# Splitting the weights of a hybrid model: half of the remainder pieces subtracted by GpSimd in the three mixers

## The chip, the cores and the metric

One of the eight cores of a Trainium2 chip runs the whole program. The metric is the device time of one execution in microseconds (us), lower is better; the times shown are medians of several runs on the chip.

## What is computed

Two stacks of layers run one after the other on a sequence of 256 tokens with 1024 features. Everything is 32-bit floating point. A layer is a feed-forward block, a mixer, and another feed-forward block:

```python
x = x + 0.5 * swiglu(rms_norm(x, ffn1_norm), w_gate, w_up, w_down)      # 1024 -> 2816 -> 1024
x = x + mixer(rms_norm(x, mix_norm), ...)
x = x + 0.5 * swiglu(rms_norm(x, ffn2_norm), w_gate, w_up, w_down)
```

The first stack has one layer, whose mixer joins a dilated attention in three groups with an RWKV-7 recurrence over 16 heads (projections, a state of 64x64 per head, normalisation, gates). The second stack has two layers, whose mixer joins three kinds of attention: with relative positions (6 heads), over the 256 best tokens by an index score (5 heads), and over a low-rank latent (5 heads). Each mixer begins with one wide projection of x and ends with a projection back to 1024 features.

## The kernel before

**Matrix products in three passes.** TensorE multiplies in a 32-bit format of reduced precision (fp32r). So each operand is written as high part plus remainder, and a product is three matmuls into the same bank: high x high, high x remainder, remainder x high (`mm3`, L1109 to L1111). The high part of the weights is `whi`, the remainder `wlo`; for the activations they are `xh`, `xl` and `yh`, `yl`.

**Chunks of weights.** The function `plan` cuts all weights into 271 chunks of at most 128 x 2048 values, in the order of use. A chunk goes through these steps:
- SP loads it into one of three buffers `raw` (L1092), as soon as the chunk three before has been split.
- ScalarE copies it, piece by piece, to `whi`, which rounds it to fp32r (L1607). `whi` and `wlo` have two buffers, so this waits until TensorE has used the chunk two before.
- VectorE subtracts, `wlo = raw - whi` (L1925), each piece as soon as ScalarE has done it.
- TensorE uses the chunk. Before its first matmul it waits for the last remainder piece of it.

A chunk is split in two pieces (in the feed-forward blocks, and where nothing is interleaved) or in four.

**The order of the work** is one list of steps, `P.steps`, built in Python by the class `Order`. Each engine walks through the same list and takes the steps for which it has a function; on one engine everything runs strictly in this order, and between engines semaphores tell when a step is done. A step `("split", i, q, n)` lets ScalarE do piece q of chunk i and VectorE subtract piece q - 1, so that VectorE's subtraction "q" is the q-th, from 1 to n. The pieces of chunk i + 1 are spread over the steps in which chunk i is used (`pump`, `pieces`).

**The other work of the mixers.** VectorE does the rotary embeddings (`rope`, L2015 to L2019, products of two tensors in SBUF), masks, row maxima, the triangular solves of the recurrence between TensorE's 64x64 products, the sums of the index scores (L2292 to L2308) and the top-k (L2318, L2321). ScalarE reads the results of matmuls out of PSUM and computes exponentials. GpSimd has the small things: it clears buffers (L2420, L2462, L2484, L2515), computes reciprocal square roots as a power (L2408, L2457, L2475), scales the gates (L2429), copies some rows (L2499 to L2509), and starts a few loads (L2418, L2443, L2468, L2481). The three mixers are the stages "mix1" and, for the second stack, "mix2" with l = 0 and l = 1; their chunks carry the owner "mix1", 0 or 1. Names of chunks such as "qkv", "gate", "in2", "uq", "ukv" are those of `plan`.

Of the kernel before, what the change touches and what calls it, by code (L numbers as in the profile page):

```python
# [291 lines left out]
class Order:  # L292


    def __init__(self, stages):
        self.chunks = plan(stages)
        self.steps = []
        self.bank = Slots(range(8))
        self.slots = {}
        self.n_dma = self.n_split = self.n_use = 0  # L300
        self.under_way = []
        for _ in range(3):
            self.feed_dma()
        self.feed_split()
        for s, st in enumerate(stages):
            if st[0] == "ffn":
                self.ffn(s, st[1])
            elif st[0] == "mix1":
                self.mix1(s)
            elif st[0] == "mix2":  # L310
                self.mix2(s, st[1])
            else:
                self.do("final", s, st[1])
        self.do("out", len(stages))
# [14 lines left out]
    def pieces(self, n):  # L329
        i = self.n_split  # L330
        if i >= len(self.chunks):
            return
        for q in range(n + 1):
            self.do("split", i, q, n)
            if q < n:
                yield 1
        self.n_split += 1
        self.feed_dma()
        yield 1
# [501 lines left out]
def build(nc, stages, x_in, wall, consts, cols, rows, lorap, ebias, out):  # L841
# [3 lines left out]
    offs = np.cumsum([0] + [128 * c[3] for c in P.chunks])  # L845
    with ExitStack() as ctx:
        M = Marks(nc, ctx)
        for name in ("pe", "act", "dve", "pool", "whi", "wlo"):
            M.add(name)
        for name in ("x", "consts", "cols", "raw0", "raw1", "raw2", "masks", "gbias", "bias0", "bias1", "lora0",  # L850
                     "lora1", "rows0", "rows1", "rows2", "gain0", "gain1", "out"):
# [131 lines left out]
        def bank_free(tile):  # L983
            return M.freed(P.bank.at[tile][1])
# [75 lines left out]
        def mus(sid):  # L1060
# [2 lines left out]
            i = "kvr".index(sid[0])  # L1063
            return [3 + 8 * i + 2 * sid[1], 4 + 8 * i + 2 * sid[1]]

        def hbuf(m):
            return yh[:, m % 5, :], yl[:, m % 5, :]

# [11 lines left out]
        def sync_program(e):  # L1080
            due = lambda *t: M.due("sp", *t)
            e.dma_start(X[:], x_in.rearrange("(t p) d -> p t d", p=128)).then_inc(*M.sig("x", ("x",)))
            e.dma_start(C[:], consts[:, 0:cbase]).then_inc(*M.sig("consts", ("c",)))
            e.dma_start(COL[:], cols).then_inc(*M.sig("cols", ("c",)))

            def load(i):
                w = P.chunks[i][3]
                src = wall[int(offs[i]):int(offs[i + 1])].rearrange("(p w) -> p w", p=128)
                if i >= 3:
                    for t in due(("wlo", ("split", i - 3))):  # L1090
                        e.wait_ge(*t)
                e.dma_start(raw[i % 3][:, 0:w], src).then_inc(*M.sig(f"raw{i % 3}", ("chunk", i)))  # L1092

            def out_(s):
                for tt in range(2):
                    for t in due(x_ready(s, tt)):
                        e.wait_ge(*t)
                    e.dma_start(out[tt * 128:(tt + 1) * 128], X[:, tt, :]).then_inc(*M.sig("out", ("out", tt)))
                for t in due(("out", ("out", 1))):
                    e.wait_ge(*t)  # L1100

            run("sp", {"load": load, "out": out_})

        def tensor_program(e):
# [30 lines left out]
            def gu(s, m, i):  # L1135
                hi, lo = whi[i % 2], wlo[i % 2]
                b = bank(("gu", s, m))
                for t in due(("wlo", ("split", i)), bank_free(("gu", s, m))):
                    e.wait_ge(*t)
                for g in range(2):  # L1140
                    for k in range(8):
# [7 lines left out]
            def rows_mm(name, acc, s, j, kk, tt, i, first, last, end, a, b, kper, *toks):  # L1149
                hi, lo = [t[:, 0:1024 * kper].rearrange("p (k n) -> p k n", k=kper) for t in (whi[i % 2], wlo[i % 2])]  # L1150
                for nn in range(2):
                    tile = (acc, s, 2 * tt + nn)
                    for t in due(("wlo", ("split", i)), first and bank_free(tile), *toks):
                        e.wait_ge(*t)
                    c = slice(nn * 512, nn * 512 + 512)
                    p = mm3(bank(tile), a, b, hi[:, kk, c], lo[:, kk, c], first, last)
# [29 lines left out]
            def proj(s, name, j, k, tt, i, nk, w, end):  # L1186
# [1 line left out]
                kk = k % nk  # L1188
                tile = (name, s, j, tt)
                c = slice(tt * 128, (tt + 1) * 128)  # L1190
                for t in due(("wlo", ("split", i)), ("dve", ("xl", s, k - k % 2)), k == 0 and bank_free(tile)):
                    e.wait_ge(*t)
                p = mm3(bank(tile)[:, 0:w], xh[:, k, c], xl[:, k, c], hi[:, kk * w:(kk + 1) * w],
                        lo[:, kk * w:(kk + 1) * w], k == 0, k == 7)
# [3 lines left out]
            def shift_mm(s, sid, j, k0, i, n, w, end):  # L1198
                b = bank(sid)
                for k in range(k0, k0 + 4):  # L1200
                    c0 = k * n * w + j * w
                    for t in due(("wlo", ("split", i)), ("dve", ("xl", s, k - k % 2)), bank_free(sid)):
                        e.wait_ge(*t)
                    p = mm3(b[0:w, j * 256:(j + 1) * 256], whi[i % 2][:, c0:c0 + w], wlo[i % 2][:, c0:c0 + w],
                            xh[:, k, :], xl[:, k, :], k == 0, k == 7)
# [263 lines left out]
            def latent_up(s, nm, tt, c0, i, end):  # L1469
                nk, k0, w, _ = latent_cols(nm)  # L1470
                cw = w if w <= 512 else w // 2
                b = bank((nm, s, tt, c0))
                for t in due(("wlo", ("split", i)), ("dve", ("lat", s, 0 if nm == "uq" else 1)),
                             bank_free((nm, s, tt, c0))):
                    e.wait_ge(*t)
                for k in range(nk):
# [434 lines left out]
        def vector_program(e):  # L1911
# [5 lines left out]
                return M.last("dve")  # L1917

            def split(i, q, n):
                if q:  # L1920
                    w = P.chunks[i][3]
                    c = slice(w * (q - 1) // n, w * q // n)
                    for t in due(("whi", ("split", i, q - 1))):
# [474 lines left out]
        def gpsimd_program(e):  # L2398
# [11 lines left out]
            def sumsq(s, tt):  # L2410
                rstd(small[:, tt:tt + 1], 1, 1024, 1e-6, ("act", ("sumsq", s, tt)), ("rstd", s, tt))

            def m1_begin(s):
                for t in due(*marked("norm", s)):
                    e.wait_ge(*t)
# [101 lines left out]
            def final(s, row):  # L2517
# [4 lines left out]
                for tt in range(2):  # L2522
                    sumsq(s, tt)

            run("pool", {"sumsq": sumsq, "m1_begin": m1_begin, "proj_out": proj_out, "rw_begin": rw_begin,
                         "r_begin": r_begin, "r_scan": r_scan, "r_nrm": r_nrm, "r_xz": r_xz, "r_yp": r_yp,
                         "r_var": r_var, "m2_begin": m2_begin, "lat_sq": lat_sq, "latent_rope": latent_rope,
                         "index_rope": index_rope, "ak_zero": ak_zero, "final": final})
# [135 lines left out]
```

## Time and profile before

| what | value |
|---|---|
| median of 3 runs | 2159.14 us (2157.56 to 2161.05) |
| the profiled execution, its own time | 2152.94 us |
| its span in the trace | 2151.1 us |
| busy: TensorE matmul / weight load | 1935.6 us (90%) / 1751.6 us (81%) |
| busy: VectorE / ScalarE / GpSimd | 1149.3 us (53%) / 927.7 us (43%) / 101.5 us (5%) |
| mean granted clock of TensorE | 0.951 of full speed |

Busy time counts from the start to the end of each instruction, also when it is held up inside. "The chain of waits" is the chain of work that ended last, followed back from the last instruction to what released each step. In the trace PE is TensorE, PEld its weight loads, DVE VectorE, ACT ScalarE, POOL GpSimd, SP the engine that issues the weight loads; "L1925" is line 1925 of the kernel before. The rows name output and inputs by the program's names, "x4" is the number of instructions merged in the row.

### The profile page before, as it was taken

The numbers are of one execution on the slowest core, as the hardware profiler recorded it, in microseconds if no ns is written. First come the engines' busy times: TensorE is split into PE (matmuls) and PEld (weight loads), VectorE is DVE, ScalarE is ACT, GpSimd is POOL, SyncE is SP. The second block draws the span as 40 slices with busy tenths as digits, with TensorE's granted clock in tenths as the row PEclk, the third lists the DMA queues.
The fourth block names the chain that finished last, engine by engine and source line by source line (L and its number), as shares of the span: only waits on it lengthen the run. The fifth ranks groups of instructions, "written<-read, shape, count | busy, mean of one in ns | idle before, by whom it ended". The sixth has DMA issues, their size and how long they took to land.

```text
span 2151.1 us, 34124 instructions
## 1 busy us (share of the span) xinstructions
PE 1935.6 (90%) x14680; PEld 1751.6 (81%) x14680; DVE 1149.3 (53%) x2096; ACT 927.7 (43%) x1681; POOL 101.5 (5%) x195
## 2 busy tenths in 40 slices
PE   6999988998878999979999778999999997779997
PEld 6998777887776899979987656999899976568997
DVE  4555545654535555555554675555555545865554
ACT  4444454422212544444444444444444445445443
POOL 0000001211110000000001100000000010000000
PEclk9999999998969999999998998999999989899999
DMA  5554524211202355535544212455455443214552
GB/s 211 186 187 166 191 95 152 94 48 46 70 4 84 138 190 185 194 131 193 180 154 138 98 59 79 157 186 186 157 186 187 166 150 118 79 40 157 177 195 108
DMA packets 42502, 296.91 MB, mean 138 GB/s; under 512 B 5120, under 2 KB 5248, under 8 KB 7792
## 3 DMA queue, kind: packets, MB, share of 16 engines
q1 hardware_dynamic: 40592, 288.38, 38.2%
q0 software_dynamic: 1760, 6.36, 1.0%
q8 instruction: 115, 1.88, 0.4%
q14 instruction: 35, 0.29, 0.0%
HBM read 293.67 MB, written 1.05 MB: 137 GB/s over the span
## 4 chain that ended last, share of the span: by engine, by line
PE 80%; DVE 13%; ACT 4%; issue 1%; POOL 1%; DMA 1%; DVEq 0%; SPq 0%; POOLq 0%; ACTq 0%
PE PS L1109 23%; PE PS L1110 23%; PE PS L1111 23%; PE PS L1129 2%; DVE wlo L1925 2%; PE PS L1373 1%; PE PS L1354 1%; DVE small L2362 1%; DVE arena L2337 1%; DVE arena L2015 1%; PE PS L1366 1%; DVE arena L2321 1%; DVE X L1970 1%; PE PS L1270 1%; ACT whi L1607 1%
## 5 line engine op out<-in xcount | busy, mean ns | idle before, releaser
L1925 DVE TENSOR_TENSOR wlo<-raw,whi 128x1024 fp32r<-128x1024 f32 (+3 forms) x684 | 658.9, 1003 | 371.6 <-ACT whi L1607 370.9
L1109 PE MATMUL PS<-xh,whi 128*128 128x256 f32 x2328 | 667.9, 287 | 0.0
L1110 PE MATMUL PS<-xl,whi 128*128 128x256 f32 x2328 | 662.6, 285 | 0.0
L1111 PE MATMUL PS<-xh,wlo 128*128 128x256 f32 x2328 | 662.2, 284 | 0.0
L1607 ACT ACTIVATE whi<-raw 128x1024 fp32r<-128x1024 f32 (+3 forms) x684 | 564.1, 874 | 216.7 <-PE PS L1111 208.2
L1109 PEld LDWEIGHTS PS<-xh,whi 128*128 128x128 f32 x2328 | 450.8, 194 | 4.4 <-issue 0.8
L1110 PEld LDWEIGHTS PS<-xl,whi 128*128 128x128 f32 x2328 | 450.8, 194 | 2.6
L1111 PEld LDWEIGHTS PS<-xh,wlo 128*128 128x128 f32 x2328 | 450.6, 194 | 0.0
L1109 PE MATMUL PS<-whi,yh 128*128 128x512 f32 (+1 forms) x628 | 246.7, 393 | 12.7 <-DVE wlo L1925 5.8
L1110 PE MATMUL PS<-wlo,yh 128*128 128x512 f32 (+1 forms) x628 | 243.9, 388 | 0.0
L1111 PE MATMUL PS<-whi,yl 128*128 128x512 f32 (+1 forms) x628 | 243.1, 387 | 0.0
L1643 ACT ACTIVATE arena<-PS 128x256 f32<-128x256 f32 x132 | 50.6, 384 | 406.0 <-PE PS L1111 406.0
L1956 DVE TENSOR_TENSOR arena<-arena,PS 128x256 f32<-128x256 f32 x132 | 55.6, 421 | 275.3 <-ACT arena L1643 275.3
L1109 PE MATMUL PS<-whi,xh 128*128 128x512 f32 (+2 forms) x432 | 180.5, 418 | 20.0 <-DVE wlo L1925 16.1
L1110 PE MATMUL PS<-wlo,xh 128*128 128x512 f32 (+2 forms) x432 | 172.1, 398 | 0.0
L1111 PE MATMUL PS<-whi,xl 128*128 128x512 f32 (+2 forms) x432 | 171.4, 397 | 0.0
L1109 PEld LDWEIGHTS PS<-whi,yh 128*128 128x128 f32 x628 | 118.3, 188 | 38.7 <-DVE wlo L1925 6.8
L1111 PEld LDWEIGHTS PS<-whi,yl 128*128 128x128 f32 x628 | 118.0, 188 | 24.5
L1110 PEld LDWEIGHTS PS<-wlo,yh 128*128 128x128 f32 x628 | 118.4, 188 | 20.6
L1109 PEld LDWEIGHTS PS<-whi,xh 128*128 128x128 f32 x432 | 89.1, 206 | 39.0 <-DVE wlo L1925 19.4
L1111 PEld LDWEIGHTS PS<-whi,xl 128*128 128x128 f32 x432 | 89.1, 206 | 17.6
L1110 PEld LDWEIGHTS PS<-wlo,xh 128*128 128x128 f32 x432 | 89.3, 207 | 14.5
(222 smaller groups left out, 1751.3 us busy)
## 6 DMA issues: line engine op xcount, KB each, us to landing
raw<-wall SPq DMA_DIRECT2D x269, 1024.0 KB, 4.8
arena<-lorap POOLq DMA_DIRECT2D x16, 128.0 KB, 2.7
arena<-ebias POOLq DMA_DIRECT2D x2, 768.0 KB, 6.8
raw<-wall SPq DMA_DIRECT2D x2, 720.0 KB, 4.2
raw<-wall SPq DMA_DIRECT2D x2, 640.0 KB, 3.9
X<-x SPq DMA_DIRECT2D x1, 1024.0 KB, 5.1
arena<-rows POOLq DMA_DIRECT2D x1, 1024.0 KB, 8.0
arena<-rows POOLq DMA_DIRECT2D x2, 512.0 KB, 3.9
```

The source lines that it names most:

```text
L1109: e.matmul(o, wa, xa, start=first, stop=False)
L1110: e.matmul(o, wa, xb, start=False, stop=False)
L1111: return e.matmul(o, wb, xa, start=False, stop=last)
L1129: i = e.transpose(b[:, c0:c0 + 128], src[:, tt, kk * 128:(kk + 1) * 128], ident)
L1270: p = e.transpose(b[:, c0 + tt * 128:c0 + tt * 128 + 128], src[:, tt * 128:tt * 128 + 128], ident)
L1354: p = e.matmul(b[ps, u * 32:(u + 1) * 32], W_.T[ps, hh, 0, tt, 0:64], some(W_.Dm[ps, u, :], k, 0), start=True, stop=True)
L1366: p = e.matmul(b[ps, u * 32:(u + 1) * 32], W_.DT[ps, u, :], some(X[ps, u, :], k, 0), start=True, stop=True)
L1373: p = e.matmul(b[ps, u * 32:(u + 1) * 32], X[ps, u, :], some(W_.DT[ps, u, :], k, 1), start=True, stop=True)
L1607: e.activation(whi[i % 2][:, c].bitcast(F32R), raw[i % 3][:, c], copy).then_inc(*M.sig("whi", ("split", i, q)))
L1643: e.activation(g, b[:, 0:256], ACT.Silu).then_inc(*M.sig("act", ("silu", s, m)))
L1925: e.tensor_tensor(wlo[i % 2][:, c], raw[i % 3][:, c], whi[i % 2][:, c].bitcast(F32), ALU.subtract).then_inc(*M.sig("wlo", ("split", i)))
L1956: e.tensor_tensor(g, g, b[:, 256:512], ALU.mult).then_inc(*M.sig("dve", ("h", s, m), ("free", ("gu", s, m))))
```

## The change

`cuts[i]`, filled in `pieces`, holds in how many pieces chunk i is cut. `on_pool(i, q)` says of each remainder piece whether GpSimd takes it: in chunks owned by a mixer, the first and, of four, the third. The piece is the same subtraction with the same operands, counted on a semaphore of its own, `wlp`. Whoever waited for `wlo` now waits for each of the two semaphores that counts pieces of that chunk: TensorE before it uses a chunk, and SP before it loads into the buffer. ScalarE's pieces and the list of steps are as before. For each engine a step of the list stands where it stood, so GpSimd meets its pieces between its own steps, in the order of the list.

```diff
+        self.cuts[i] = n
...
+        def on_pool(i, q):
+
+            return P.chunks[i][0] in ("mix1", 0, 1) and q % 2 == 1
+
+        def split_done(i):
+            who = {"wlp" if on_pool(i, q) else "wlo" for q in range(1, P.cuts[i] + 1)}
+            return [(w, ("split", i)) for w in sorted(who)]
...
                 if i >= 3:
-                    for t in due(("wlo", ("split", i - 3))):
+                    for t in due(*split_done(i - 3)):
                         e.wait_ge(*t)
...
-                for t in due(("wlo", ("split", i)), bank_free(("gu", s, m))):
+                for t in due(*split_done(i), bank_free(("gu", s, m))):
                     e.wait_ge(*t)
...
             def split(i, q, n):
-                if q:
+                if q and not on_pool(i, q):
...
+            def split(i, q, n):
+                if q and on_pool(i, q):
+                    w = P.chunks[i][3]
+                    c = slice(w * (q - 1) // n, w * q // n)
+                    for t in due(("whi", ("split", i, q - 1))):
+                        e.wait_ge(*t)
+                    e.tensor_tensor(wlo[i % 2][:, c], raw[i % 3][:, c], whi[i % 2][:, c].bitcast(F32), ALU.subtract
+                                    ).then_inc(*M.sig("wlp", ("split", i)))
```

The waits of the other five kinds of matrix steps of TensorE change as that of "gu" does.

GpSimd's instructions at the start of the first mixer, before the change. They load and clear buffers once the norm is done, then scale the gates:

```order
L2418 DMA arena<-consts 128x384 [waits dve,pool,act,pe]
L2418 DMA arena<-consts 128x768
L2419 DMA arena<-rows 128x2048
L2420 MEMSET arena 128x3072
L2421 MEMSET arena 128x2
L2429 TENSOR_SCALAR GATE<-GATE 128x512 [waits act] x8
```

The same place after the change (its line numbers are a little higher):

```order
L2436 DMA arena<-consts 128x384 [waits dve,pool,act,pe]
L2436 DMA arena<-consts 128x768
L2437 DMA arena<-rows 128x2048
L2438 MEMSET arena 128x3072
L2439 MEMSET arena 128x2
L2428 TENSOR_TENSOR wlo<-raw,whi 128x256 [waits whi] x2
L2428 TENSOR_TENSOR wlo<-raw,whi 128x512 [waits whi] x18
L2428 TENSOR_TENSOR wlo<-raw,whi 128x1024 [waits whi]
L2428 TENSOR_TENSOR wlo<-raw,whi 128x512 [waits whi] x4
L2447 TENSOR_SCALAR GATE<-GATE 128x512 [waits act] x2
```

Between the clearing and the gates now stand 25 pieces, those of the lora, the qkv and the first three gate chunks; the first of them are behind the clearing.

GpSimd's instructions from the start of a later mixer to the latents, before:

```order
L2484 MEMSET arena 128x1280
L2487 MEMSET arena 64x64 [waits pool]
L2488 MEMSET arena 64x64
L2405 TENSOR_SCALAR small<-small 128x2 [waits act]
L2408 TENSOR_TENSOR small<-small,C 128x2 [waits pool]
L2405 TENSOR_SCALAR small<-small 128x2 [waits act]
L2408 TENSOR_TENSOR small<-small,C 128x2 [waits pool]
L2499 COPY arena<-arena 128x5x64 [waits act]
```

And after:

```order
L2506 MEMSET arena 64x64
L2428 TENSOR_TENSOR wlo<-raw,whi 128x1024 [waits whi]
L2428 TENSOR_TENSOR wlo<-raw,whi 128x512 [waits whi] x8
L2414 TENSOR_SCALAR small<-small 128x2 [waits act]
L2417 TENSOR_TENSOR small<-small,C 128x2 [waits pool]
L2414 TENSOR_SCALAR small<-small 128x2 [waits act]
L2417 TENSOR_TENSOR small<-small,C 128x2 [waits pool]
L2428 TENSOR_TENSOR wlo<-raw,whi 128x512 [waits whi] x2
L2428 TENSOR_TENSOR wlo<-raw,whi 128x360 [waits whi] x2
L2428 TENSOR_TENSOR wlo<-raw,whi 128x640 [waits whi]
L2428 TENSOR_TENSOR wlo<-raw,whi 128x1024 [waits whi]
L2517 COPY arena<-arena 128x5x64 [waits act]
```

The first piece of "in2 8" (1024 columns) now stands directly behind the clearing, and the two small operations that give the scale of the latents directly ahead of the pieces of "in2 7", "uq", "ukv" and "in2 4".

VectorE at the same latents, before: the pieces of "in2 7" around the scaling of the latents (L2261), their remainders (L1944), the pieces of "uq", "ukv", "in2 4", and the ropes:

```order
L2261 TENSOR_SCALAR arena<-arena,small 128x384 [waits pool]
L2261 TENSOR_SCALAR arena<-arena,small 128x256 [waits pool]
L1925 TENSOR_TENSOR wlo<-raw,whi 128x512 [waits whi] x3
L1944 SCALAR_TENSOR_TENSOR yl<-PS,COL,yh 128x256 [waits act]
L1944 SCALAR_TENSOR_TENSOR yl<-PS,COL,yh 128x256
L1944 SCALAR_TENSOR_TENSOR yl<-PS,COL,yh 128x256 [waits act] x2
L1944 SCALAR_TENSOR_TENSOR yl<-PS,COL,yh 128x256
L1925 TENSOR_TENSOR wlo<-raw,whi 128x360 [waits whi] x4
L1925 TENSOR_TENSOR wlo<-raw,whi 128x640 [waits whi] x2
L1925 TENSOR_TENSOR wlo<-raw,whi 128x1024 [waits whi] x2
L2015 TENSOR_TENSOR arena<-arena,C 128x16 [waits dve,pe]
```

After:

```order
L2270 TENSOR_SCALAR arena<-arena,small 128x384 [waits pool]
L2270 TENSOR_SCALAR arena<-arena,small 128x256 [waits pool]
L1934 TENSOR_TENSOR wlo<-raw,whi 128x512 [waits whi] x2
L1953 SCALAR_TENSOR_TENSOR yl<-PS,COL,yh 128x256 [waits act]
L1953 SCALAR_TENSOR_TENSOR yl<-PS,COL,yh 128x256
L1953 SCALAR_TENSOR_TENSOR yl<-PS,COL,yh 128x256 [waits act] x2
L1953 SCALAR_TENSOR_TENSOR yl<-PS,COL,yh 128x256
L1934 TENSOR_TENSOR wlo<-raw,whi 128x360 [waits whi] x2
L1934 TENSOR_TENSOR wlo<-raw,whi 128x640 [waits whi]
L1934 TENSOR_TENSOR wlo<-raw,whi 128x1024 [waits whi]
L2024 TENSOR_TENSOR arena<-arena,C 128x16 [waits dve,pe]
```

Nothing else moves on VectorE: half of the pieces are gone, the rest stands where it stood.

## Rows read from the trace of the kernel before

**Rows 1.** windows of two mixers: length, busy time of each engine, clock, DMA
```profile
216.00:723.00 507.00, 442.14 (x4952) 384.17 (x4950) 268.76 (x641) 178.29 (x389) 61.72 (x99) 0.93 0.26 91
...
1128.00:1340.00 212.00, 172.48 (x834) 142.65 (x832) 125.32 (x345) 98.85 (x254) 11.24 (x26) 0.87 0.27 92
```

**Rows 2.** the page, part 4: shares of the chain by engine
```profile
PE 80%; DVE 13%; ACT 4%; issue 1%; POOL 1%; DMA 1%; DVEq 0%; SPq 0%; POOLq 0%; ACTq 0%
```

**Rows 3.** groups by line and form on VectorE: busy us, mean ns, idle before
```profile
L1925 DVE TENSOR_TENSOR wlo<-raw,whi 128x1024 fp32r<-128x1024 f32 x412 | 486.4, 1222 | 223.2 <-ACT whi L1607 222.8
...
L1925 DVE TENSOR_TENSOR wlo<-raw,whi 128x512 fp32r<-128x512 f32 x252 | 163.6, 686 | 136.9 <-ACT whi L1607 136.6
```

**Rows 4.** groups by line and form on GpSimd
```profile
L2450 POOL TENSOR_SCALAR arena<-arena,small 128x256 f32<-128x256 f32 x8 | 10.5, 1318 | 74.4 <-DVE arena L2096 51.6 <-ACT arena L1724 22.3 <-ACT arena L1737 0.5
...
L2429 POOL TENSOR_SCALAR GATE<-GATE 128x512 f32<-128x512 f32 x8 | 4.9, 618 | 135.1 <-ACT GATE L1656 135.1
```

**Rows 5.** timeline, VectorE and GpSimd, 1191 to 1196 us: start, length, what
```profile
1191.35 0.17 DVE L2019 TENSOR_TENSOR arena<-arena 128x16 f32<-128x16 f32 x1
...
1195.59 0.47 DVE L2019 TENSOR_TENSOR arena<-arena 128x16 f32<-128x16 f32 x1
...
1195.59 0.45 POOL L2499 COPY arena<-arena 128x320 f32<-128x320 f32 x1
```

**Rows 6.** timeline of one qkv chunk: remainders, and TensorE's first matmul of that chunk
```profile
241.79 2.19 ACT L1607 ACTIVATE whi<-raw 128x512 fp32r<-128x512 f32 x4
...
242.45 2.50 DVE L1925 TENSOR_TENSOR wlo<-raw,whi 128x512 fp32r<-128x512 f32 x4 [3.85 <-ACT whi L1607]
...
246.06 0.39 PE L1109 MATMUL PS<-whi,xh 128*128 128x512 f32 x1
```

**Rows 7.** timeline, the last gate chunk
```profile
352.13 2.50 DVE L1925 TENSOR_TENSOR wlo<-raw,whi 128x512 fp32r<-128x512 f32 x4 [1.22 <-ACT whi L1607]
...
354.86 0.39 PE L1109 MATMUL PS<-whi,xh 128*128 128x512 f32 x1
```

**Rows 8.** timeline and chain, latents of the first later mixer
```profile
1166.81 0.70 POOL L2408 TENSOR_TENSOR small<-small,C 128x2 f32<-128x2 f32 x1
...
1168.20 2.04 DVE L1925 TENSOR_TENSOR wlo<-raw,whi 128x512 fp32r<-128x512 f32 x3
...
1181.67 1.57 DVE wlo L1925 x2
...
1189.66 1.22 DVE wlo L1925
```

**Rows 9.** timeline, GpSimd's clearing and TensorE's first use, last mixer
```profile
1745.14 0.14 POOL L2488 MEMSET arena<- 64x64 f32 x1
...
1745.75 0.77 PE L1109 MATMUL PS<-whi,xh 128*128 128x512 f32 x1
```

**Rows 10.** timeline of GpSimd and chain, start of the first mixer
```profile
223.03 0.12 POOL L2421 MEMSET arena<- 128x2 f32 x1
...
225.49 2.42 DVE wlo L1925 x4
```

**Rows 11.** chain of waits, ropes and merge of the first mixer
```profile
279.90 1.18 DVE arena L2015 x4
...
689.76 1.60 DVE wlo L1925 x3
```

**Rows 12.** groups of VectorE in the recurrence; chain there and in the top-k
```profile
L1996 DVE SCALAR_TENSOR_TENSOR arena<-arena,COL 128x256 f32<-128x256 f32 x22 | 9.7, 482 | 0.4
...
L2077 DVE TENSOR_TENSOR GATE<-GATE 128x512 f32<-128x512 f32 x4 | 2.8, 692 | 0.1
...
523.81 0.60 DVE wlo L1925
...
1253.10 2.30 DVE GATE L2292
```

More of the change, by code:

```diff
@@ L298, in __init__ @@
         self.bank = Slots(range(8))
-        self.slots = {}
+        self.slots, self.cuts = {}, {}
         self.n_dma = self.n_split = self.n_use = 0
@@ L847, in build @@
         M = Marks(nc, ctx)
-        for name in ("pe", "act", "dve", "pool", "whi", "wlo"):
+        for name in ("pe", "act", "dve", "pool", "whi", "wlo", "wlp"):
             M.add(name)
@@ L1152, in rows_mm @@
                     tile = (acc, s, 2 * tt + nn)
-                    for t in due(("wlo", ("split", i)), first and bank_free(tile), *toks):
+                    for t in due(*split_done(i), first and bank_free(tile), *toks):
                         e.wait_ge(*t)
@@ L1190, in proj @@
                 c = slice(tt * 128, (tt + 1) * 128)
-                for t in due(("wlo", ("split", i)), ("dve", ("xl", s, k - k % 2)), k == 0 and bank_free(tile)):
+                for t in due(*split_done(i), ("dve", ("xl", s, k - k % 2)), k == 0 and bank_free(tile)):
                     e.wait_ge(*t)
@@ L1201, in shift_mm @@
                     c0 = k * n * w + j * w
-                    for t in due(("wlo", ("split", i)), ("dve", ("xl", s, k - k % 2)), bank_free(sid)):
+                    for t in due(*split_done(i), ("dve", ("xl", s, k - k % 2)), bank_free(sid)):
                         e.wait_ge(*t)
@@ L1472, in latent_up @@
                 b = bank((nm, s, tt, c0))
-                for t in due(("wlo", ("split", i)), ("dve", ("lat", s, 0 if nm == "uq" else 1)),
+                for t in due(*split_done(i), ("dve", ("lat", s, 0 if nm == "uq" else 1)),
                              bank_free((nm, s, tt, c0))):
@@ L2523, in final @@
                     sumsq(s, tt)
-            run("pool", {"sumsq": sumsq, "m1_begin": m1_begin, "proj_out": proj_out, "rw_begin": rw_begin,
+            run("pool", {"split": split, "sumsq": sumsq, "m1_begin": m1_begin, "proj_out": proj_out, "rw_begin": rw_begin,
                          "r_begin": r_begin, "r_scan": r_scan, "r_nrm": r_nrm, "r_xz": r_xz, "r_yp": r_yp,
```

## The prediction, made before the changed kernel was run

> **What bounds the kernel now.** I read the busy times of the mixer stretches first, then the chain of waits, then, chunk by chunk, when a chunk's last remainder is ready and when TensorE first uses it. [rows 1] show the first mixer (216 to 723 us) and the first of the two later ones (1128 to 1340); the third reads like the second. TensorE is busy 442.1 of 507 us and 172.5 of 212 us, so what can be won or lost there is some 65 and 40 us of idle time, plus whatever a new wait adds. VectorE is busy 53% and 59%, GpSimd 12% and 5%. By this view GpSimd is free. Over the whole span TensorE is 80% of the chain and VectorE 13% [rows 2]. The remainders as such are thus not the bound. They matter at the places where TensorE waits for a chunk, and where VectorE's own row is the chain.
>
> **What the change moves.** In the three mixers there are 284 remainder pieces; 142 (q = 1 and 3) go to GpSimd: 122 of 512 columns, 10 of 1024, 10 smaller. On VectorE a piece of 512 takes 0.686 us and one of 1024 1.222 us [rows 3]: about 122 x 0.68 + 10 x 1.22 = 95 us less busy time. ScalarE's part, TensorE's work and all transfers stay the same in number; SP's loads wait for one semaphore more, two chunks ahead of need.
>
> **The price of a piece on GpSimd** is not in the trace: it has no subtraction of two wide tensors there. Nearest is its one-input operation on 128x512, 0.618 us [rows 4]; a second input can be free (bound 0.62) or cost a second pass (2 x 0.618 = 1.24). The other way lies its operation on 128x256 with a per-partition scalar, 1.318 us, twice that for 512 columns, 2.6 us [rows 4]. I take 1.2 us, and 2.4 for 1024: same width, two reads. The Trainium skill (GPSIMD Engine Reference, section 3.1) gives 4497 ns for 2048 fp32 columns, by which a piece would be an estimated 1.1 to 1.2 us, and the sum would stay as below; no run here shows it yet.
>
> **The port.** [rows 5]: a 16-column subtraction of VectorE takes 0.17 us at 1191.35 and 0.47 us at 1195.59, exactly where GpSimd's copy of 0.45 us began at the same moment. I read it so: a VectorE instruction that reads two SBUF tensors and a GpSimd instruction that reads SBUF don't run together; the second waits for the first to end. Every remainder piece is such an instruction, on both engines. So two pieces of one chunk run one after the other: no parallel gain at all. The Trainium skill (SBUF — State Buffer, section Who interferes with whom) states the same as a rule, an exclusive lock for the whole instruction, and the trace agrees (0.17 against 0.47 us). It speaks against this change: without it, a chunk's remainders would be ready about as early as now.
>
> Worked out for a chunk of four pieces [rows 6]: ScalarE starts at 241.79 and has a piece ready every 0.55 us; VectorE does 242.45 to 244.95; TensorE takes the chunk at 246.06, 1.11 us later. After: GpSimd q1 242.6 to 243.8, VectorE q2 to 244.45, GpSimd q3 to 245.65, VectorE q4 to 246.3. That is **1.3 us later**. Two pieces of 1024: GpSimd 2.4, then VectorE 1.2, also 1.3 us later.
>
> **The sum.**
> 1. Steady chunks. In the projections the margin alternates, 2.0 and 1.1 us. Only the 1.1 ones lose: 0.2 us each, five of them, 1.0. The last gate chunk has 0.23 us (VectorE ends 354.63, TensorE starts 354.86 [rows 7]): 1.1. Together +2.1.
> 2. The latents of each later mixer, where TensorE already waits for the last piece [rows 8]. Chunk "in2 7": GpSimd is busy until 1167.5 with the small operation, then q1, and the scaling on VectorE and three remainder pieces that end at 1170.24 queue behind the port: +1.3. "ukv": 2 x 640 columns, 1.5 + 0.8 from 1181.85 against an end of 1183.24: +0.9. "in2 4": +1.3, since VectorE's ropes follow on the chain straight behind (1190.88). 3.5 per mixer, +7.0.
> 3. GpSimd's own queue, first come first served. At the start of a mixer it waits for the norm, then clears buffers. In the last mixer this ends at 1745.28; q1 of "in2 8" (1024 columns) stands behind it and ends at 1747.6, and TensorE wants it at 1745.75 [rows 9]: +1.9. In the mixer before, TensorE comes to that chunk later, behind the clearing by more than the piece takes: no loss. In the first, the clearing ends at 223.15 [rows 10]; both lora pieces and q1 of the first qkv chunk come behind it, and block VectorE's token shift. Its remainders end at 227.91 now, the chain goes through them, and I put +0.9. Together +2.8.
> 4. Where a piece on GpSimd gets in between two-input operations of VectorE that are the chain and no piece was in the way before: the ropes of the first mixer from 279.90 [rows 11], +1.2. Ahead of the merge four pieces follow each other on the chain, 689.76 to 692.26 [rows 11], +1.3. Together +2.5.
> 5. The recurrence, 384 to 700 us. Gain: pieces q1 or q3 on the chain, at 401.30, 483.47, 523.81 and 556.90 (the third is in [rows 12]), 4 x 0.6 = -2.4. Loss: 29 GpSimd pieces among some 147 two-input operations of VectorE in 316 us, 0.47 per us (16 groups of the view by line, from L1996 with 22 to L2077 with 4, [rows 12]). An estimate: half the pieces hit one and hold it 0.7 us, 10 us of VectorE, a third of it on the chain, +3. GpSimd's 24 small operations of the recurrence stand behind a piece now and then, inside that estimate. Together +0.6.
> 6. Index scores and top-k. Here VectorE is the chain almost without a gap, and half of its pieces go away: five x 0.6 per mixer = -3.0. Against it stand the adds over 128x2048 (2.30 us, [rows 12]) and their followers, all with two inputs: each GpSimd piece between them costs 1.2, two in the last one and a third of one (0.4) in the first: +2.8. -0.2 per mixer, about 0.
>
> Sum 2.1 + 7.0 + 2.8 + 2.5 + 0.6 + 0 = **+15 us**. The profiled execution took 2152.94 us with a span of 2151.1; it becomes 2168. The median of the three runs is 6.2 us above that execution, so the forecast against the median is 2159.14 + 15 = **2174 us**.
>
> **Where it is late next.** TensorE stalls shift ScalarE's evictions and the next chunk alike, so a stall of 0.2 us is not paid twice. The loads have three buffers and run a whole chunk ahead of ScalarE; that chunk's work hides them, and I cost them at nothing. If that cover went, a load would cost what the remainder came late, 1.3 us.
>
> **Rivals.**
> - A, faster: GpSimd gives way, or reads so that the port is free for most of a piece. For it: only one meeting in which VectorE came second stands in [rows 5], and its copy reads one tensor, so the hold by a long piece is argued from a short one. Against it: the 0.47 us. Then terms 1, 2 and 4 vanish, 3 stays (+2.8), and 5 and 6 keep their gains, -2.4 - 6.0 and the copies that no longer wait for a piece, -1: -6.6, about 2152.5. It decides from the point where the holds of terms 4 to 6 are below 0.25 us each. Chance 0.10.
> - B, no difference (within 4.3 us, 0.2%, about what a measurement of this kernel can tell from no change): the piece costs 0.8 us or less. Then a chunk is 2 x 0.4 us less late, +0.5 us: term 1 falls to 0.3, 2 to 3.0, 3 to 1.5, 4 to 1.3, 5 to -0.9 and 6 to -2.2, together +3, 2162. For it: nothing in the rows excludes a second input at no cost. Chance 0.16.
> - C, much slower: the piece costs 2.6 us. Then q4 ends 2 x 1.4 = 2.8 us later than in my case, 4.1 later than now; some 20 steady chunks with margins of 1.1 or 2.0 stall for 2 to 3 us, 50, and terms 2 to 4 double, +12: about 2236. Chance 0.08.
> - Forecast (1.2 us, lock in force), 2163.5 to 2192: 0.66.
>
> **Range.** 2158 to 2192. Its low end takes in most of B, the high end holds pieces of 1.5 us (0.6 us more at each of the six places of term 1, six of term 2 and two of term 4, 8; 4 more in 3, 5 and 6: 2186), and a third hit more often than I put it in 5 and 6. Left out are A and C. Faster 0.10, same 0.16, slower 0.74.
>
> **What the profile after would show.** A group of 142 on GpSimd near 1.2 us for 512 columns. Remainders on VectorE whose duration splits in two, 0.68 and up to 1.9 us. q4 of a qkv chunk ending within 0.3 us of TensorE's first use. A TensorE wait of about 2 us for GpSimd near 1745. VectorE busy time in the mixers that falls by less than 95 us, since blocked time counts as busy. I am wrong if two pieces overlap freely, if the piece is far from 1.2 us, or if GpSimd's small operations in the recurrence (the powers that VectorE waits for) prove to be the chain.

## The result, and the profile after

| | before | after |
|---|---|---|
| median of 4 runs each, us | 2160.1 | 2198.45 (2194.38 to 2201.85) |
| ratio | | 1.0178 (1.0157 to 1.0198) |
| span of the profiled execution | 2151.1 | 2192.2 |
| busy: TensorE / VectorE / GpSimd, us | 1935.6 / 1149.3 / 101.5 | 1959.3 / 1156.8 / 308.5 |
| mean granted clock of TensorE | 0.951 | 0.940 |

38 us slower, where I forecast 15. In all that follows, +9 lines: L1925 is now L1934, L1996 is L2005; GpSimd's pieces are L2428. The groups of pieces by line and form (busy us, mean ns, idle before), GpSimd's and VectorE's, and the token-shift mix:

```profile
L2428 POOL TENSOR_TENSOR wlo<-raw,whi 128x512 fp32r<-128x512 f32 x122 | 174.5, 1443 | 335.8 <-ACT whi L1616 335.6
L2428 POOL TENSOR_TENSOR wlo<-raw,whi 128x1024 fp32r<-128x1024 f32 x10 | 23.8, 2379 | 221.2 <-ACT whi L1616 221.2
...
L1934 DVE TENSOR_TENSOR wlo<-raw,whi 128x1024 fp32r<-128x1024 f32 x402 | 485.7, 1249 | 228.5 <-ACT whi L1616 228.1
L1934 DVE TENSOR_TENSOR wlo<-raw,whi 128x512 fp32r<-128x512 f32 x130 | 142.9, 1122 | 134.7 <-ACT whi L1616 134.7
L2005 DVE SCALAR_TENSOR_TENSOR arena<-arena,COL 128x256 f32<-128x256 f32 x27 | 21.2, 823 | 0.5
```

142 pieces left VectorE and its busy time rose by 7.5 us: what is left is held so long (512 columns: 1122 ns against 686 in [rows 3]; the mix: 823 against 482) that the relief is gone. A steady chunk of four, in the timeline (start, length; answers to [rows 6]):

```profile
243.56 2.19 ACT L1616 ACTIVATE whi<-raw 128x512 fp32r<-128x512 f32 x4
244.26 3.00 POOL L2428 TENSOR_TENSOR wlo<-raw,whi 128x512 fp32r<-128x512 f32 x2 [4.70 <-ACT whi L1616]
244.74 3.07 DVE L1934 TENSOR_TENSOR wlo<-raw,whi 128x512 fp32r<-128x512 f32 x2 [4.63 <-ACT whi L1616]
...
247.87 0.50 PE L1118 MATMUL PS<-whi,xh 128*128 128x512 f32 x1
```

Two engines at work, and the remainders end 4.25 us (247.81 less 243.56) behind ScalarE's start, where VectorE alone needed 3.16 (244.95 less 241.79, [rows 6]): one after the other, 1.1 us later. It costs next to nothing here, since TensorE still comes just behind. The recurrence is where it costs. VectorE, ScalarE and GpSimd at one mix of it:

```profile
421.08 0.60 ACT L1676 ACTIVATE arena<-PS 128x512 f32<-128x512 f32 x1 [1.39 <-PE PS L1120]
421.58 1.14 ACT L1616 ACTIVATE whi<-raw 128x512 fp32r<-128x512 f32 x2
...
421.72 0.69 DVE L2000 TENSOR_TENSOR arena<-arena 128x512 f32<-128x512 f32 x1 [0.53 <-ACT arena L1676]
422.44 1.78 DVE L2005 SCALAR_TENSOR_TENSOR arena<-arena,COL 128x256 f32<-128x256 f32 x2
...
422.28 1.27 POOL L2428 TENSOR_TENSOR wlo<-raw,whi 128x512 fp32r<-128x512 f32 x1 [1.55 <-ACT whi L1616]
```

The last matmul of a projection releases both ScalarE's copy for the mix and, because it frees a weight buffer, the next high piece. GpSimd's piece starts 0.6 us behind the mix, and the mix's last two instructions, 0.88 us together, take 1.78. This meeting occurs at four of the twelve projections of the recurrence (382.33, 403.33, 421.72 and 440.52); at two more (393.69, 531.73) a piece that came at another moment holds the mix, and at six nothing does. In the list of steps the piece stands behind the mix; VectorE would have kept that order, GpSimd has nothing to wait for and overtakes.

Where the profiled execution lost its 41.1 us, by TensorE's first use of each chunk. Its matmuls are counted in order, and the time of a matmul before is taken from its time after; the last column is the step of the prediction:

| stretch | lost, us | forecast |
|---|---|---|
| to the first qkv chunk | 2.1 | 0.9 (term 3) |
| qkv chunks (nine) | 0.3 | 1.0 (term 1) |
| gate chunks, with the ropes | 2.2 | 1.1 + 1.2 (1, 4) |
| "up" chunk | 1.7 | 0 |
| recurrence, v 0 to wout 0 | 11.3 | 0.6 (term 5) |
| wout and wo chunks | 3.4 | 1.3 (term 4) |
| latents, in2 6 to in2 5, two mixers | 6.4 + 6.5 | 3.5 + 3.5 (term 2) |
| scores, top-k and the rest, two mixers | 0.6 + 3.5 | 0 + 0 (term 6) |
| in2 12 to in2 8, last mixer | 2.9 | 1.9 (term 3) |
| all else | 0.2 | 0 |

### The profile page after: what moved, and what is told of

It reads as the page before. It is cut to its first block, busy times and chain, and to the rows that moved or that the text cites. A ratio compares the mean times of both kernels' runs of the same rounds, so it can differ in the third digit from the quotient of the medians.

```text
span 2192.2 us, 34249 instructions
## 1 busy us (share of the span) xinstructions
PE 1959.3 (89%) x14680; PEld 1770.4 (81%) x14680; DVE 1156.8 (53%) x1954; ACT 928.1 (42%) x1681; POOL 308.5 (14%) x337
## 4 chain that ended last, share of the span: by engine, by line
PE 80%; DVE 12%; ACT 4%; issue 2%; POOL 1%; DMA 1%; DVEq 0%; SPq 0%; POOLq 0%; ACTq 0%
PE PS L1118 23%; PE PS L1119 22%; PE PS L1120 22%; PE PS L1138 2%; DVE wlo L1934 1%; PE PS L1382 1%; DVE arena L2024 1%; PE PS L1363 1%; PE PS L1375 1%; ACT whi L1616 1%; DVE arena L2346 1%; DVE small L2371 1%; PE PS L1128 1%; DVE X L1979 1%; PE PS L1279 1%
## 5 line engine op out<-in xcount | busy, mean ns | idle before, releaser
L1934 DVE TENSOR_TENSOR wlo<-raw,whi 128x1024 fp32r<-128x1024 f32 (+1 forms) x542 | 636.7, 1211 | 376.2 <-ACT whi L1616 375.7
L2428 POOL TENSOR_TENSOR wlo<-raw,whi 128x512 fp32r<-128x512 f32 (+3 forms) x142 | 208.6, 1480 | 954.6 <-ACT whi L1616 954.5
```

Of the source, the lines that this page charges most:

```text
L1934: e.tensor_tensor(wlo[i % 2][:, c], raw[i % 3][:, c], whi[i % 2][:, c].bitcast(F32), ALU.subtract).then_inc(*M.sig("wlo", ("split", i)))
L2428: e.tensor_tensor(wlo[i % 2][:, c], raw[i % 3][:, c], whi[i % 2][:, c].bitcast(F32), ALU.subtract).then_inc(*M.sig("wlp", ("split", i)))
```

## The experiments

Each was timed in five rounds beside the kernel before. Three of them do without part of the remainders or replace it by other values; it is said there.

**Where.** Two kernels share the change between them.

```diff
-            return P.chunks[i][0] in ("mix1", 0, 1) and q % 2 == 1
+            return P.chunks[i][0] == "mix1" and P.chunks[i][1] in ("k", "v", "r") and q % 2 == 1
```

> GpSimd takes its pieces only in the twelve k, v and r chunks of the recurrence; everywhere else VectorE keeps all of them. Theory T1 (collisions on the port that are not random: ScalarE makes a piece of the high part directly behind the eviction that starts VectorE's next link of the chain, so GpSimd's piece starts together with that link and holds it by about 0.9 us each): nearly the whole loss of the recurrence seen in the changed kernel, chunk 52 to 65, comes back here, +10 to +14 us against before, with VectorE's two-input groups (128x256 with a column, 128x512) held as there. Theory T2 (the recurrence was only pushed around by what came before it, the projections): the loss needs the other changes, +0 to +4 us. My prediction on record, hits at random, would say +0.6.

> The complement: GpSimd takes its pieces everywhere in the three mixers except in the k, v and r chunks. If the stages add up (both theories that put the cost at the piece itself): +24 to +29 us against before. If the recurrence's loss is only a consequence of lateness brought in from the projections, it shows here too and this kernel is near the full +38. My terms on record without the recurrence sum to +14.6.

Measured: 1.0059 (1.0037 to 1.0081), +12.7 us, and 1.0109 (1.0093 to 1.0126), +23.6 us, just below the +24 that I expected. The two add up to 36, nearly the whole. 23 pieces of 142 (22 of 512 columns, one of 1024) carry a third of the loss, without any lateness brought in from elsewhere; T2 is out. The first number is a middle of two groups: three executions took 2165.7 to 2168.2 us at a mean granted clock of 0.946 to 0.948, three took 2176.2 to 2178.2 us at 0.940 to 0.942. One kernel thus costs 6 to 18 us, and the clock goes with the difference.

**Is it the port, or the queue and the length?** GpSimd writes a constant in place of the subtraction; and, for the value of the relief alone, the pieces are given to nobody.

```diff
-                    e.tensor_tensor(wlo[i % 2][:, c], raw[i % 3][:, c], whi[i % 2][:, c].bitcast(F32), ALU.subtract
-                                    ).then_inc(*M.sig("wlp", ("split", i)))
+                    m = max(1, (c.stop - c.start) // 64 + (360 == c.stop - c.start) * 3)
+                    for j in range(m):
...
+                        p = e.memset(wlo[i % 2][:, cc].bitcast(F32), 1e-5)
+                    p.then_inc(*M.sig("wlp", ("split", i)))
```

> GpSimd has the same pieces at the same places of its queue, behind the same waits, but does not compute them: it writes a constant into the piece in 64-column strips, some 1.2 to 1.3 us for 512 columns, and reads nothing. (So this part of the weights' remainders is left out of the result.) Port theory T1: an operation that reads nothing from SBUF does not hold VectorE, so only the length of the piece and GpSimd's queue are left: VectorE's remainder pieces fall back to 0.69 us and the 128x256 group to 0.48, time -4 to +6 us against before. Queue and length theory T3 (the loss is that a GpSimd piece ends later and that its small operations stand behind it): nothing changes, +30 to +40.

> VectorE leaves the same 142 pieces to nobody: they are not computed at all (the buffers keep old values there), and GpSimd is as before. It shows what the relief of VectorE alone is worth. Pieces of VectorE on the chain sum to 33 us in the trace of before over three mixers, about half of them of the kind that goes away: -10 to -15 us against before, if TensorE or something else does not take the place. If the relief is worth nothing (TensorE is the bound there anyway): within 3 us. The difference between this kernel and the write-only one is what length and queue cost without the port.

Measured: write-only 0.9962 (0.9947 to 0.9977), -8.2 us, faster than T1's own range; left out 0.9918 (0.9904 to 0.9932), -17.7, more than the 10 to 15 that I expected. VectorE's pieces in the write-only kernel, by form, and one written piece of 512 columns, eight strips:

```profile
L1934 DVE TENSOR_TENSOR wlo<-raw,whi 128x512 fp32r<-128x512 f32 x130 | 88.9, 689 | 165.3 <-ACT whi L1616 165.3
...
396.88 0.76 POOL L2431 MEMSET wlo<- 128x64 f32 x8 [9.09 <-ACT whi L1616]
```

Not one of VectorE's pieces is held. So the relief is worth 18 us, and a queue of short pieces takes back 9.5 of it (-17.7 against -8.2). The other 47 us (from -8.2 to +38.4) can't be put down to the reading of SBUF by this kernel alone: a written piece takes 0.72 to 0.76 us, not the 1.2 to 1.3 that I expected, so GpSimd's pieces are shorter here as well. The next kernel separates the two.

**What in GpSimd's instruction holds VectorE?** One input instead of two, and two halves instead of one piece.

```diff
-                    e.tensor_tensor(wlo[i % 2][:, c], raw[i % 3][:, c], whi[i % 2][:, c].bitcast(F32), ALU.subtract
+                    e.tensor_scalar(wlo[i % 2][:, c], raw[i % 3][:, c], 1e-5, None, ALU.mult
```

> The changed kernel with GpSimd's subtraction replaced by an operation with one input, the weights times 1e-5 (this part of the remainders is thus left out of the result), 0.62 us for 512 columns in the trace of before. It reads from SBUF, but half as long. Port theory T1 (what reads from SBUF holds VectorE, for as long as it lasts): VectorE is still held, by 0.62 us instead of 1.29; a chunk is ready 0.1 us later than in the kernel before; +2 to +12 us against before, and VectorE's remainder group shows a second level near 1.2 us. If only a second input of GpSimd makes the conflict: like the write-only kernel or better, -8 to -14, remainder group at 0.69 throughout.

> The changed kernel with each GpSimd piece made of two instructions of half the columns (256 mostly, about 0.7 us each). If the hold lasts for one instruction and VectorE comes in between: held operations of VectorE wait 0.6 instead of up to 1.3 us, the chunk is done about as late as before, +28 to +38 us against before. If VectorE does not come in between two GpSimd instructions that follow each other (one of its pieces lasted 3.23 us at 565.36, through two GpSimd pieces and a clearing): same holds, and 0.1 us more for each piece, +38 to +44.

Measured: one input 1.0038 (1.0024 to 1.0053), +8.2 us; halves 1.0132 (1.0115 to 1.0149), +28.5. The time of the first is in my range, but for another reason. GpSimd and VectorE at one chunk of it:

```profile
236.01 2.95 POOL L2428 TENSOR_SCALAR wlo<-raw 128x512 fp32r<-128x512 f32 x2 [0.26 <-ACT whi L1616]
...
236.48 0.69 DVE L1934 TENSOR_TENSOR wlo<-raw,whi 128x512 fp32r<-128x512 f32 x1 [1.06 <-ACT whi L1616]
237.53 1.10 DVE L1934 TENSOR_TENSOR wlo<-raw,whi 128x512 fp32r<-128x512 f32 x1 [0.35 <-ACT whi L1616]
```

The operation takes 1.49 us, not 0.62. A VectorE piece that starts 0.47 us into it is not held at all; one that starts 0.06 us behind the second is held by 0.4 us, not by the 1.4 that were left. In 33 of the 36 held pieces of 512 columns the hold ends 0.46 to 0.50 us after GpSimd's start, whether VectorE came 0.06 or 0.30 us behind it. In the changed kernel, by contrast, the hold lasts to within 0.14 us of the end of GpSimd's piece, in 59 of 60 held pieces of 512 columns: at 244.74 VectorE comes 0.48 us into a piece of 1.30 and takes 1.37 instead of 0.69. So this GpSimd instruction with one input holds VectorE for its first 0.47 us, the one with two inputs nearly to its end; the second level I expected near 1.2 us lies at 1.10 for that reason.

This also parts length from hold. GpSimd's pieces are longer here than in the changed kernel (1.49 us against 1.27 to 1.30 unheld) and stand at the same places of its queue, and the time is 30 us less (+8.2 against +38.4). T3 is out: those 30 us are the price of the long hold. In the halves kernel VectorE's 512-column group has a mean of 818 ns against 1122: it does come in between two instructions, and the chunks are still done late, since two halves take 1.77 us in the mean (884 ns each, held themselves) against 1.44 for a whole piece.

**Is it the overtaking?** GpSimd waits for the mix ahead of its piece.

```diff
+            def shift_mix(s, sid, n, w):
+                mixed[:] = [("dve", ("mix", sid))]
...
-                    for t in due(("whi", ("split", i, q - 1))):
+                    for t in due(("whi", ("split", i, q - 1)), *mixed):
```

> As the kernel with the k, v and r chunks alone, but GpSimd's piece waits in addition for VectorE's token-shift mix that stands ahead of the piece in the list of steps (the place at which VectorE would take the piece itself). In the trace of the changed kernel ScalarE's copy for that mix and its first high piece of the next chunk are released by the same matmul, and GpSimd's piece starts some 0.6 us behind the start of the mix and holds its last link for 0.9 us, at 383.05, 422.43, 441.23 and in other places. Theory T1 (timed collisions): the links are free again, the loss of +12.7 us shrinks to +2 to +7 us. If the loss is one of many small hits spread over all of VectorE's two-input work: it stays at +10 to +13 us.

Measured: 1.0001 (0.9990 to 1.0013), better than the +2 to +7 us that I expected. All of the +12.7 us is gone, with the same 23 pieces on the same engine. The mix's group by form, and GpSimd and VectorE at the mix shown above:

```profile
L2005 DVE SCALAR_TENSOR_TENSOR arena<-arena,COL 128x256 f32<-128x256 f32 x27 | 11.9, 482 | 0.5
```

```profile
414.44 0.88 DVE L2005 SCALAR_TENSOR_TENSOR arena<-arena,COL 128x256 f32<-128x256 f32 x2
...
415.47 1.28 POOL L2433 TENSOR_TENSOR wlo<-raw,whi 128x512 fp32r<-128x512 f32 x1 [2.73 <-DVE arena L2005]
```

In the changed kernel nine of 27 links are held; now none is. Behind the mix come operations with an input in PSUM, and the piece runs beside them.

**Then place decides.** Three kernels give GpSimd only pieces chosen by what VectorE does at their place. The first two take the same 16, with and without a wait for the end of the index sums.

```diff
-            return P.chunks[i][0] in ("mix1", 0, 1) and q % 2 == 1
+            own, kind, j = P.chunks[i][:3]
+            return own in (0, 1) and ((kind, j) == ("wout2", 2) or (kind, j, q) == ("in2", 3, 4)
+                                      or (kind, j) == ("in2", 0) and q < 4)
...
-                    for t in due(("whi", ("split", i, q - 1))):
+                    for t in due(("whi", ("split", i, q - 1)), P.chunks[i][1] == "wout2" and
+                                 ("dve", ("ixm", stages.index(("mix2", P.chunks[i][0])), 1))):
```

> GpSimd takes only 8 pieces of 512 columns in each later mixer, all where VectorE walks through the top-k, whose operations (maximum, replacement) the trace shows unheld beside a piece at 1254.18, 1260.63 and 1264.44: the last piece of the in2 3 chunk, the first three of in2 0, and all four of the wout2 2 chunk, which wait in addition until the index scores are summed. Nothing in the first mixer. Theory T1 (a piece costs only where VectorE needs its second input from SBUF): about 8 x 0.6 us less on a stretch where VectorE is the chain, less some that TensorE takes over, -3 to -4 us per mixer, -5 to -9 in all against before. Theory T4 (anything given to GpSimd holds VectorE or comes too late): 0 to +6 us.

> The same 16 pieces as in the picked kernel, without the extra wait: GpSimd starts the pieces of wout2 2 as soon as ScalarE has made the high part, which is while VectorE sums the index scores (two inputs from SBUF, 128x2048 in 2.30 us). Theory T1 (place decides, not number): the first two or three pieces run with the sums, hold them by 1.3 us each and are stretched themselves (2.5 us at 1281.12 in the changed kernel): +1.3 to +2.6 us per mixer against the picked kernel, so -3 to -6 against before instead of -8.8. If only the number of pieces taken from VectorE counted: the same -8.8.

Measured: 0.9959 (0.9944 to 0.9973), -8.8 us; without the wait 0.9994 (0.9983 to 1.0004), -1.3 us, worse than the -3 to -6 that I expected. With the wait, four GpSimd pieces and VectorE beside them (of the 16 rounds of the top-k the first):

```profile
1257.42 4.95 POOL L2431 TENSOR_TENSOR wlo<-raw,whi 128x512 fp32r<-128x512 f32 x4 [18.43 <-DVE small L2381]
...
1257.72 0.43 DVE L2329 MAX8 small<-arena 128x8 f32<-128x256 f32 x1
1258.19 0.09 DVE L2332 MATCH_VALUE_LOAD arena<-small,arena 128x8 f32 x1
1258.27 0.41 DVE L2332 MATCH_REPLACE8 arena<-small,arena 128x256 f32<-128x256 f32 x1
```

Without it, the same four pieces and the sums of the index scores:

```profile
1259.30 7.82 POOL L2430 TENSOR_TENSOR wlo<-raw,whi 128x512 fp32r<-128x512 f32 x4 [14.30 <-ACT whi L1618]
...
1258.37 2.29 DVE L2303 TENSOR_TENSOR GATE<-GATE,small 128x2048 f32<-128x2048 f32 x1
1260.70 2.19 DVE L2307 TENSOR_TENSOR GATE<-GATE 128x1024 f32<-128x1024 f32 x1
1262.92 1.66 DVE L2315 TENSOR_TENSOR GATE<-GATE 128x512 f32<-128x512 f32 x1
1264.61 1.38 DVE L2319 TENSOR_TENSOR arena<-GATE 128x256 f32<-128x256 f32 x1
```

Beside the top-k nothing is longer than in the kernel before (0.43 and 0.41). In the sums three links took 2.19, 1.66 and 1.38 us, against 1.23, 0.69 and 0.42 in the picked kernel: 2.9 us of hold for 2.4 us of relief.

The third adds seven pieces of the recurrence, each behind the scaling of the keys:

```diff
+        behind = {("v", 1, 1): 1, ("v", 1, 2): 1, ("r", 2, 3): 3, ("r", 2, 4): 3, ("v", 3, 1): 4, ("r", 3, 3): 5,
+                  ("r", 3, 4): 5}
...
+            if own == "mix1":
+                return (kind, j, q) in behind
...
+                    if own == "mix1":
+                        late = "dve", ("rk", behind[kind, j, q])
```

> The picked kernel and seven pieces of the recurrence besides (v 1 first and second, r 2 and r 3 third and fourth, v 3 first), those that the chain of before shows as VectorE's own pieces right behind the scaling of the keys; GpSimd waits for that scaling, and behind it VectorE has only operations with an input from PSUM, or is idle for 2 to 4 us. Theory T1: no hold, about 7 x 0.6 us = 4.2 us leave VectorE's chain there, half to all of it on the path: -11 to -13 us against before. If GpSimd's pieces delay its own clearing of buffers, or anything else of VectorE, as much as they give: -6 to -9, like the picked kernel or worse.

Measured: 0.9936 (0.9922 to 0.9949), -13.8 us by the ratio, median 2147.83 against 2159.82, where I expected -11 to -13. This is the fastest kernel of the study that computes everything, with 23 pieces on GpSimd in place of 142. Its interval touches that of the picked kernel, which ran beside other runs of before; that the seven pieces are worth 5 us is likely, not shown.

## Why the prediction was wrong

**Right.** The direction, the price of a piece (1.27 to 1.30 us unheld against 1.2 taken, 2.38 against 2.4), and the serial run of the two pieces of a chunk (1.1 us later against 1.3). The lost-parallelism argument, that the port takes all of the gain, held; rivals A, B and C are out by the price and by the holds. The last gate chunk cost 1.0 against 1.1; the ropes 1.0 against 1.2; in the latents the three waits I named cost 1.2, 0.7 and 1.1 against 1.3, 0.9 and 1.3. VectorE's busy time fell by less than 95 us, as forecast: it did not fall at all.

The loss has two parts, and the prediction priced only one. Between the first and the last matmul, TensorE's idle time and its busy time grew as follows (us, from the same matmuls before and after; the stretches are those of the first table, but for small shifts of their bounds):

| stretch | idle, more | matmuls, longer | forecast |
|---|---|---|---|
| to the first qkv chunk | -0.8 | 2.6 | 0.9 |
| qkv chunks | 1.0 | -0.8 | 1.0 |
| gate chunks, ropes | 1.6 | 0.7 | 2.3 |
| "up" chunk | 0.0 | 1.6 | 0 |
| recurrence | 5.1 | 6.3 | 0.6 |
| wout and wo chunks | 1.7 | 1.0 | 1.3 |
| latents, two mixers | 3.4 + 3.4 | 3.1 + 3.0 | 3.5 + 3.5 |
| scores, top-k and the rest, two mixers | 1.7 - 0.4 | -0.9 + 4.0 | 0 |
| in2 12 to in2 8, last mixer | 0.0 | 2.8 | 1.9 |
| all | 16.8 | 23.7 | 15 |

The waits came to 16.8 us against a forecast of 15, but that nearness is partly luck: the recurrence has 4.5 more than forecast, and the start of the first mixer and term 3 of the last one have no longer wait at all.

**The step that failed most: a stall was taken to cost its own length.** The prediction put nothing for matmuls that take longer, and gave no reason. TensorE's 14680 matmuls were busy 1935.6 us before and 1959.3 after, at a mean granted clock of 0.951 and 0.940. From v 0 to the use of r 2 (windows over the same chunks, before and after: length, busy times, clock third from the end):

```profile
375.22:495.57 120.35, 108.50 (x1582) 98.38 (x1581) 74.28 (x189) 41.72 (x100) 19.80 (x31) 0.93 0.21 76
```

```profile
381.48:512.36 130.88, 113.92 (x1582) 103.66 (x1581) 74.07 (x175) 41.62 (x100) 38.36 (x45) 0.88 0.21 71
```

Of 10.5 us lost there, 5.4 are matmuls that took longer at a granted clock of 0.88 instead of 0.93, more of the time at the 1.2 GHz level, and 5.1 are waits. How much of the longer matmuls the change caused is not settled. The kernel without the wait, which moves nothing in the recurrence, shows half of it in the same chunks:

```profile
374.91:498.09 123.18, 111.11 (x1583) 100.82 (x1581) 74.28 (x189) 41.72 (x100) 19.80 (x31) 0.90 0.21 74
```

Nor does the sum of the waits decide it: in the one-input kernel TensorE is idle 3.8 us less than before in all, and its matmuls take 16.7 us more; its whole loss is of this kind. In the profiled executions the clock is 0.953 picked and 0.954 left out, 0.940 to 0.942 in the slow kernels and the one-input kernel. That longer or more frequent waits lower the clock agrees with most of these runs; no run tests it by itself.

**Wrong: term 5, the recurrence.** It is 11 of the 26 us that are missing. The step that failed for the waits is the sentence "half the pieces hit one and hold it 0.7 us, 10 us of VectorE, a third of it on the chain": a hit rate for pieces and chain as if they were independent. Some of them are released by the same matmul. From 381.5 to 721 us VectorE's operations took 16.9 us more than the median of the same operations before, and 8.3 of that is in the mixes, which TensorE waits for. TensorE's idle time from v 0 to wout 0 grew from 43.1 to 48.0 us; it is 48.0 as well with the recurrence alone, 43.0 when GpSimd waits for the mix, and 43.1 when the recurrence keeps all its pieces. The kernel that only restores the order gives everything back (1.0001), so this is shown.

**Wrong by its size: term 2, the latents,** 12.9 us against 7.0. The waits themselves came out as forecast, 3.4 us per mixer against 3.5. What was missing is again the matmuls. In the "in2 7" chunk TensorE, after a wait that had grown, runs six matmuls of 0.43 us where they had been 0.23, and at the end of "in2 4" six more:

```profile
1192.81 0.43 PE PS L1119
1193.24 0.43 PE PS L1120
...
1195.79 0.23 PE PS L1119
```

Inside the waits one was missed: at 1220.55 a rope of 0.23 us takes 1.29, because the first piece of the *next* chunk, in2 5, starts at 1220.45. This is the reverse of the overtaking. VectorE had done that piece at its place in the list, ahead of these ropes (1194.36 before); on GpSimd it stands behind four small copies that wait for VectorE's first ropes, and so comes late into the second ones:

```profile
1219.76 0.72 POOL L2527 COPY arena<-arena 128x32 f32<-128x32 f32 x4 [2.59 <-DVE arena L2028]
1220.45 1.29 POOL L2428 TENSOR_TENSOR wlo<-raw,whi 128x512 fp32r<-128x512 f32 x1
...
1220.55 1.29 DVE L2024 TENSOR_TENSOR arena<-arena,C 128x80 f32<-128x80 f32 x1
```

**Term 3, last mixer.** It came out near in size (2.9 against 1.9), but not for the reason given; that is luck. GpSimd is done at 1774.7 and TensorE comes at 1776.2, so nothing waits. The in2 12 chunk took 10.2 us instead of 7.4, at a clock of 0.50 instead of 0.71 as the windows of that stretch show. All ten experiments have the same 10.2 us there, also those that move no piece near it: the execution of before that was profiled was lucky by 2.8 us. The "up" chunk may be of the same kind: it took 5.5 us before and 7.1 after, 7.2 with the pieces left out, and 6.9 and 7.0 in two kernels that move nothing ahead of it (the recurrence alone and the last picked one), but 5.5 to 5.6 in three others that move nothing there either. At least 2.8 us of the table are therefore not the change's; against the medians the loss is 38.

**Term 6.** The two mixers lost 0.6 and 3.5 us against nothing forecast. Two kernels that move nothing there, the recurrence alone and the one behind the mix, differ from the profiled execution of before by -2.8 us in the first and +3.2 to +3.4 in the second. The second's 3.5 us are thus no more the change's than in2 12's, and the change costs about 3.5 in the first. That the exchange of relief for holds comes out near zero agrees with the kernel without the wait (-1.3 us in all). I have not traced the wout and wo chunks, 3.4 us against 1.3, nor the start of the first mixer, 2.1 against 0.9, beyond the split in the table above.

**The range** left no room for this: its high end gave 6 us to more frequent hits in terms 5 and 6, none of its cases had the holds in step with the chain, and none had a slower matmul.

## What to carry to other kernels

Work given to a second engine that shares a port with the first isn't only slower or faster: it leaves the first engine's order. Ask what releases the moved piece and what the same event releases on the other engine, and make it wait for the operation it would collide with; 23 pieces went from +12.7 us to 0 by that wait alone. Choose the pieces by their neighbours (operations with an input from PSUM, searches over one tensor, an idle stretch), not by their number: 23 well placed gave -13.8 us, 142 gave +38. And don't take a stall on TensorE at its own length: here 16.8 us of longer waits came with 23.7 us of longer matmuls.

## What the runs showed of the hardware

- **The hold depends on the form of both instructions.** VectorE's subtraction of two SBUF tensors is held to within 0.14 us of the end by a GpSimd subtraction of two, for the first 0.47 us by a multiply with one input that takes 1.49, and not at all by a constant written. The Trainium skill (SBUF — State Buffer, Who interferes with whom) says that two SBUF inputs on VectorE contend with a GpSimd instruction that reads, not with one that only writes: this agrees (689 ns beside writes). It calls the shared pair an exclusive lock, and says of VectorE's two-port modes that it is held for the whole instruction; I had read that into the two-input case as well. For one input on GpSimd it does not hold (a piece unheld 0.47 us into 1.49). My reading of [rows 5] from a copy of 0.45 us could not have told the two apart.
- **A fast one-input copy of VectorE is held by writes too.** Its 128x256 copy takes 0.28 us; in the write-only kernel one took 2.20 us, through three pieces' worth of strips:

```profile
385.74 2.20 DVE L2121 COPY arena<-arena 128x256 f32<-128x256 f32 x1
...
385.66 2.13 POOL L2431 MEMSET wlo<- 128x64 f32 x24
```

- **VectorE may lose the port again and again.** After the change one piece of 0.68 us lasted 3.23, through two GpSimd pieces with a clearing of buffers between them, though 0.2 us lay between the pieces. It does not always go so: in the steady chunk shown above and in the halves kernel VectorE comes in between two GpSimd pieces; what decides stays open.

```profile
565.24 1.31 POOL L2428 TENSOR_TENSOR wlo<-raw,whi 128x512 fp32r<-128x512 f32 x1
566.48 0.32 POOL L2480 MEMSET arena<- 128x256 f32 x1
566.76 1.27 POOL L2428 TENSOR_TENSOR wlo<-raw,whi 128x512 fp32r<-128x512 f32 x1
...
565.36 3.23 DVE L1934 TENSOR_TENSOR wlo<-raw,whi 128x512 fp32r<-128x512 f32 x1
```

- **GpSimd's one-input multiply that rounds to fp32r takes 1.49 us for 512 columns,** longer than its two-input subtraction (1.29), where a one-input operation from f32 to f32 takes 0.62 [rows 4]. The two differ in the output format, in the tensors and in the operation (the row of 0.62 multiplies and adds, in place); no run separates them. The bounds in the prediction came from that row; for a piece with this output it was too low.
